# A decoder layer on one core: transfers of the attention merge issued by ScalarE, the sine product as one VectorE operation, merge work inside the waits for powers

## The chip, the cores and the metric

The kernel runs on one core of a Trainium2 chip. The metric is the device time of one execution in microseconds. Of the kernel before there are three timed runs, and one more execution that the hardware profiler recorded.

## The reference

One decoder layer over 1024 tokens of width 1024, float32. The part that matters here is mixer A, a dilated window attention with 12 query heads in three groups over 4 key/value heads:

```
qa = apply_rope(rmsnorm(qa, qn_a), cos, sin) * (HEAD_DIM_A ** -0.5)
ka = apply_rope(rmsnorm(ka, kn_a), cos, sin)
def apply_rope(t, cos, sin):
    t1, t2 = jnp.split(tf, 2, axis=-1)
    return concatenate([t1 * cos - t2 * sin, t2 * cos + t1 * sin])
for g, (window, dilation) in enumerate(((128,1), (512,4), (2048,16))):
    o, lse = dilated_group(q[:, :, g], k, v, window, dilation)
w = softmax(stack(lses), axis=0)
o = sum(w[..., None] * stack(outs), axis=0)
```

The last two lines are the merge: the three groups' outputs of a key/value head, weighted by their softmax denominators. Mixer B is a gated linear attention; both are projected, gated and added, and a SwiGLU block follows.

## The kernel before

All matrix products of float32 data are made of three products of a high and a low part (lines 2228 to 2230, helper `three`), so every weight tile is cast by ScalarE (`hi_a`, L992) and its rest taken by VectorE (`lo_a`, L1527). The program is written out for each engine, in order, with semaphores between them; a loop `Fori(1, H)` runs the attention of heads 1 to 3, and head 0 is written ahead of it.

An attention head is 16 slots, `s` = 0 to 15. In slots 0 to 7 TensorE makes a tile of q and k for four (token tile, column) pairs (`four`), in 8 to 15 it makes gate columns (`stream`). The tile of slot j goes this way:

- ScalarE squares its four parts with sums (L1077, in `act_head_a`).
- VectorE turns the sums into variances (L1679, `qk_norm`), GpSimd raises them to the power -0.5 (L730, `pool_rope`), VectorE multiplies the tile by power and gain into `qg` (L1692).
- Rotation: VectorE multiplies by the cosines (L1667) and one half by the sines (L1668), GpSimd the other half by the sines (L734); VectorE subtracts and adds (L1672, L1673).
- TensorE transposes the rotated tile behind slot j + 2 (L2367, called T(j) below), and ScalarE copies it to `qk_t` (L1095, L1098), behind its squares of slot j + 2.

From slot 6 on, the scores of a pair of blocks, their masks and negated maxima on VectorE (L1707, L1711), exponentials on ScalarE (L1119), transposes (L2328) and products with v (L2342) are put between (`UNITS_AT`).

Head h merges head h - 1 meanwhile. Its steps are: GpSimd stores the statistics to DRAM (L743) and loads them in eight small transfers in token order (`merge_stats`, L749 to L754), ahead of the power of slot 0; VectorE takes differences in slot 1 (`merge_diffs`, from L1623), ScalarE exponentials (L1065), VectorE normalises behind slot 3 (`merge_norm`); GpSimd stores the weights (L763) and, once they are stored, loads them into `wb` on all partitions (L767), between the powers of slots 3 and 4 (`merge_weights`); VectorE multiplies `wb` by the outputs (`merge_mul`, L1655) in slot 5 and twice in slot 8; GpSimd adds the three (L772, L774) and stores the sum (`merge_sum`). Head 3 is merged in the first head of mixer B, `pool_head(0, False)`.

The waits that tie the loads down are these two, and each is a wait of GpSimd's queue, with the powers behind it:

```
pool.wait_ge(stat_out, 16 * h + 16)
pool.wait_ge(wgt_out, 16 * h + 16)
```

Of the kernel before, what the change touches and what calls it, by code (L numbers as in the profile page):

```python
# [19 lines left out]
ALU = mybir.AluOpType  # L20
# [3 lines left out]
P = 128  # L24
# [10 lines left out]
def decoder_layer(nc, x_d, pos_d, norm1_d, w_in_d, qn_d, kn_d, w_up_d, b_a_d, gn_d, w_pa_d, w_pb_d,  # L35
# [256 lines left out]
    t1_gain, t1_cos, t1_sin, rot_done = sem("t1_gain"), sem("t1_cos"), sem("t1_sin"), sem("rot_done")  # L292
# [65 lines left out]

    def leave_phase(eng):
        eng.drain().then_inc(phase_end, 1)  # L360
# [11 lines left out]

    def by_tile(t, j, d=P):

        return t.rearrange("p (t m) d -> p t m d", m=2) if len(QK[j][0]) == 2 else t
# [301 lines left out]
    def _(pool):  # L677
# [60 lines left out]
        def merge_stats(h):  # L738

            sd = stat_d[bass.ds(h, 1)].rearrange("a u q -> (a u) q")  # L740
            pool.wait_ge(stat_sbd, h + 1)
            alone(pool)
            pool.dma_start(sd, stat_sb[:, :]).then_inc(stat_out, 16)  # L743
            pool.wait_ge(stat_out, 16 * h + 16)
            pool.wait_ge(c_wgt, 3 * h)
            alone(pool)
            for q in range(2):
                r0 = NU * q
                pool.dma_start(st8[:, q, 0, :], sd[r0:r0 + 8, :]).then_inc(stat_in, 16)  # L749
                for b in range(2):  # L750
                    pool.dma_start(st8[4 * b:4 * b + 4, q, 1, :].rearrange("c (r jl) -> c r jl", jl=32),
                                   sd[r0 + 8 + b:r0 + 16:2, :].rearrange("r (jh jl) -> jh r jl", jl=32)
                                   ).then_inc(stat_in, 16)
                pool.dma_start(st8[:, q, 2, :].rearrange("c (r il) -> c r il", il=16),  # L754
                               sd[r0 + 16:r0 + 24, :].rearrange("r (ih il) -> ih r il", il=16)
                               ).then_inc(stat_in, 16)

        def merge_weights(h):

            pool.wait_ge(c_wgt, 3 * h + 3)  # L760
            alone(pool)
            wd = wgt_d[bass.ds(h, 1)].rearrange("a g c t -> (a g) c t")
            pool.dma_start(wd.rearrange("g c t -> c g t"), e8[:, :, :]).then_inc(wgt_out, 16)  # L763
            pool.wait_ge(wgt_out, 16 * h + 16)
            pool.wait_ge(oa_out, 16 * h)
            alone(pool)
            pool.dma_start(wb[:, :, :], wd.rearrange("g c t -> g (c t)").partition_broadcast(P)  # L767
                           ).then_inc(wb_in, 16)
# [10 lines left out]
        for j in range(8):  # L779
            pool_rope(0, j)  # L780
# [33 lines left out]
        def pool_head(h, tail):  # L814
# [29 lines left out]
            else:  # L844
                work = ["d0", "W0", "d1", "d2", "S0", "d3"] + last
            for w in work:
# [6 lines left out]
                elif w[0] == "W":  # L853
                    merge_weights(H - 1)
# [129 lines left out]
    def _(act):  # L984
# [82 lines left out]
        def act_head_a(h, behind):  # L1067
# [4 lines left out]
            for s in range(16):  # L1072
# [26 lines left out]
                for j in UNITS_AT.get(s, []):  # L1099
# [36 lines left out]
        def act_head(h, tail):  # L1136
# [33 lines left out]
            for s in range(2 * TB):  # L1170
# [346 lines left out]
    def _(dve):  # L1517
# [139 lines left out]
        def dve_head_a(h, behind):  # L1657
            def rope(j):
# [6 lines left out]
                else:  # L1665
                    out, src = (t.rearrange("p m (a f) -> p (m a) f", a=2) for t in (r, qg[:, :, :]))
                dve.tensor_tensor(out, src, table(cos_t, j, 2), ALU.mult).then_inc(t1_cos, 1)  # L1667
                dve.tensor_tensor(by_tile(rs[:, :, 64:128], j), by_tile(qg[:, :, 0:64], j), table(sin_t, j, 1),  # L1668
                                  ALU.mult).then_inc(t1_cos, 1)
                dve.wait_ge(t1_cos, 2 * n + 2)  # L1670
                dve.wait_ge(t1_sin, n + 1)
                dve.tensor_tensor(r[:, :, 0:64], r[:, :, 0:64], rs[:, :, 0:64], ALU.subtract).then_inc(rot_done, 1)  # L1672
                dve.tensor_tensor(r[:, :, 64:128], r[:, :, 64:128], rs[:, :, 64:128], ALU.add).then_inc(rot_done, 1)  # L1673

            def qk_norm(j):
# [12 lines left out]
                dve.wait_ge(t1_sin, n)  # L1688
# [981 lines left out]
```

## Time and profile before

| | |
|---|---|
| Runs timed | 1890.19, 1892.96, 1894.15 us (median 1892.96) |
| The profiled execution | 1892.71 us |
| Its span | 1891.2 us, 27575 instructions |
| TensorE busy | 1797.0 us, 95% of the span |
| VectorE busy | 1101.1 us, 58% |
| ScalarE busy | 700.6 us, 37% |
| GpSimd busy | 551.1 us, 29% |
| Mean granted clock of TensorE | 0.99 |

The span is the time between the first and the last instruction of the profiled execution, 1.5 us less than its own time. Engines are named PE (TensorE), DVE (VectorE), ACT (ScalarE), POOL (GpSimd) and SP in the rows; L12 is a line of the kernel. A time in brackets is how long the engine stood idle before an instruction, and the arrow names what released it. Busy shares are means over stages with different limits.

### The profile page before, as it was taken

How to read it: one execution, taken by the hardware profiler on the slowest of the kernel's cores; microseconds unless marked ns; L12 is line 12 of the kernel's file. 1: busy time of each engine (PE TensorE's matmuls, PEld its weight loads, DVE VectorE, ACT ScalarE, POOL GpSimd, SP SyncE). 2: the span in 40 equal slices, each digit the busy share in tenths (PEclk: the TensorE clock that was granted, in tenths of full speed). 3: DMA queues.
4: the chain of work that ended last, by engine and by line, in shares of the span. 5: the costliest groups of instructions: out<-in, count | busy, mean ns of one | idle time of the engine just before them, and what ended most of it. 6: DMA issues, size and time to landing. Idle time of an engine off the chain costs nothing. (4 is left out here: it accounts for less than half of the span.)

```text
span 1891.2 us, 27575 instructions
## 1 busy us (share of the span) xinstructions
PE 1797.0 (95%) x9188; PEld 1521.5 (80%) x9188; DVE 1101.1 (58%) x1928; ACT 700.6 (37%) x1598; POOL 551.1 (29%) x654
## 2 busy tenths in 40 slices
PE   6999989999989899999997999999999999999999
PEld 6888877878877888888895888877888888888887
DVE  5362462562652966667576554587555555566786
ACT  5233233233243335353536222453333333334443
POOL 2020230320412705151412000006565555620120
PEclk9999999999999899999999999999999999999999
DMA  7311321421221211111015323214232323178764
GB/s 201 100 35 50 91 95 34 116 74 61 79 78 46 68 46 46 35 33 55 28 72 197 120 83 112 101 67 134 94 105 100 116 89 111 70 251 318 257 213 171
DMA packets 169173, 196.42 MB, mean 104 GB/s; under 512 B 9488, under 2 KB 119344, under 8 KB 168576
## 3 DMA queue, kind: packets, MB, share of 16 engines
q1 hardware_dynamic: 154832, 156.59, 25.9%
q0 software_dynamic: 7984, 28.29, 4.5%
q10 hardware_dynamic: 6272, 10.49, 1.5%
q8 instruction: 43, 0.70, 0.1%
q14 instruction: 42, 0.34, 0.1%
HBM read 150.88 MB, written 44.45 MB: 103 GB/s over the span
## 5 line engine op out<-in xcount | busy, mean ns | idle before, releaser
L2228 PE MATMUL bank<-act_hi,w_hi 128*128 128x512 f32 x568 | 229.1, 403 | 3.9 <-DVE act_lo L1862 3.6
L2230 PE MATMUL bank<-act_hi,w_lo 128*128 128x512 f32 x568 | 222.8, 392 | 0.0
L2229 PE MATMUL bank<-act_lo,w_hi 128*128 128x512 f32 x568 | 222.2, 391 | 0.0
L2228 PE MATMUL bank<-ca,wq 128*128 128x512 f32 x528 | 206.9, 392 | 6.7 <-DVE wq L1973 4.3
L2230 PE MATMUL bank<-ca,wq 128*128 128x512 f32 x528 | 206.0, 390 | 0.0
L2229 PE MATMUL bank<-ca,wq 128*128 128x512 f32 x528 | 205.9, 390 | 0.0
L2228 PE MATMUL bank<-w_hi,act_hi 128*128 128x256 f32 (+1 forms) x576 | 181.3, 315 | 4.0 <-DVE act_lo L1543 3.1
L2229 PE MATMUL bank<-w_lo,act_hi 128*128 128x256 f32 (+1 forms) x576 | 177.7, 308 | 0.0
L2230 PE MATMUL bank<-w_hi,act_lo 128*128 128x256 f32 (+1 forms) x576 | 177.6, 308 | 0.0
L2228 PEld LDWEIGHTS bank<-act_hi,w_hi 128*128 128x128 f32 x568 | 107.6, 189 | 27.6 <-DVE act_lo L1862 4.8
L2230 PEld LDWEIGHTS bank<-act_hi,w_lo 128*128 128x128 f32 x568 | 107.2, 189 | 23.2
L2229 PEld LDWEIGHTS bank<-act_lo,w_hi 128*128 128x128 f32 x568 | 107.5, 189 | 20.9
L2228 PEld LDWEIGHTS bank<-ca,wq 128*128 128x128 f32 x528 | 99.5, 188 | 29.8 <-issue 3.7
L1527 DVE TENSOR_TENSOR w_lo<-w_raw,w_hi 128x1024 fp32r<-128x1024 f32 x38 | 46.1, 1223 | 126.6 <-ACT w_hi L992 126.6
L2228 PEld LDWEIGHTS bank<-w_hi,act_hi 128*128 128x128 f32 x576 | 111.0, 193 | 9.4 <-issue 3.3
L2230 PEld LDWEIGHTS bank<-ca,wq 128*128 128x128 f32 x528 | 99.4, 188 | 20.7
L2229 PEld LDWEIGHTS bank<-ca,wq 128*128 128x128 f32 x528 | 99.5, 188 | 20.6
L2230 PEld LDWEIGHTS bank<-w_hi,act_lo 128*128 128x128 f32 x576 | 111.0, 193 | 5.2
L2229 PEld LDWEIGHTS bank<-w_lo,act_hi 128*128 128x128 f32 x576 | 111.1, 193 | 4.9
L1973 DVE TENSOR_TENSOR wq<-wr,wq 128x512 fp32r<-128x512 f32 x66 | 69.9, 1059 | 70.1 <-ACT wq L1361 70.1
L1361 ACT CAST wq<-tq 128x512 fp32r<-128x512 f32 x88 | 54.3, 620 | 140.2 <-PE bank L2230 118.0
L922 POOL TENSOR_TENSOR yq<-yq,sg 128x512 f32<-128x512 f32 x33 | 53.1, 1609 | 147.5 <-DVE yq L2135 59.7
(364 smaller groups left out, 4295.1 us busy)
## 6 DMA issues: line engine op xcount, KB each, us to landing
w_raw<-in_w_in SPq DMA_DIRECT2D x60, 512.0 KB, 4.0
rawd<-in_w_ffn_down SPq DMA_DIRECT2D x99, 256.0 KB, 5.0
rx<-y_scratch SPq DMA_DIRECT2D x77, 256.0 KB, 4.3
wr<-in_w_ffn_gate SPq DMA_DIRECT2D x11, 1024.0 KB, 5.5
wr<-in_w_ffn_up SPq DMA_DIRECT2D x11, 1024.0 KB, 5.4
y_scratch<-sq SPq DMA_DIRECT2D x11, 1024.0 KB, 4.3
y_scratch<-yq SPq DMA_DIRECT2D x33, 256.0 KB, 2.1
gate_scratch<-gbuf ACTq DMA_DIRECT2D x32, 256.0 KB, 2.1
```

Of the source, the lines that this page charges most:

```text
L922: pool.tensor_tensor(yq(k), yq(k), sg[:, k, :], ALU.mult).then_inc(ym_done, 1)
L1361: act.copy(wq_hi[:, w_slot(p, j), :].rearrange("p (kt n) -> p kt n", n=P), src).then_inc(whi_done, 1)
L1527: dve.tensor_tensor(w_lo[:, slot, :], w_raw[:, slot, :], w_hi[:, slot, :].bitcast(F32), ALU.subtract).then_inc(lo_done, 1)
L1973: dve.tensor_tensor(lo, src, hi.bitcast(F32), ALU.subtract).then_inc(wlo_done, 1)
L2228: pe.matmul(ps, lhs_hi, rhs_hi, start=first, stop=False, skip_group_check=onto)
L2229: pe.matmul(ps, lhs_hi, rhs_lo, start=False, stop=False, skip_group_check=onto)
L2230: return pe.matmul(ps, lhs_lo, rhs_hi, start=False, stop=last, skip_group_check=onto)
```

## The change

- The store and the eight loads of the statistics, the store of the weights and their broadcast load are issued by ScalarE: the store behind the copy that ends a head, the loads behind the squares of slot 0, the others at the end of slots 4 and 5. For head 3: in slots 0, 2 and 3 of the first head of mixer B.
- The sine product is one VectorE operation over both halves, written to `rs` in place; the subtraction and the addition read its crossed halves. GpSimd keeps the powers and the sums.
- The normalisation moves from behind the rotation of slot 3 to the wait for its power; the products from slots 5, 8, 8 to the waits in slots 6 and 7 and to slot 8.

```diff
+    def load_stats(eng, h):
+        sd = stat_d[bass.ds(h, 1)].rearrange("a u q -> (a u) q")
+        eng.wait_ge(stat_out, 16 * h + 16)
+        eng.wait_ge(c_wgt, 3 * h)
...
+    def load_weights(eng, h):
+        eng.wait_ge(wgt_out, 16 * h + 16)
+        eng.wait_ge(oa_out, 16 * h)
...
-        def pool_rope(h, j):
+        def pool_rstd(h, j):
             n = 8 * h + j
             pool.wait_ge(t1_var, n + 1)
             pool.tensor_tensor(qk_st[:, 0, j, :], qk_st[:, 1, j, :], mhalf[:, 0:4],
                                ALU.pow).then_inc(t1_rstd, 1)
-            pool.wait_ge(t1_gain, 4 * n + 4)
-            pool.wait_ge(rot_done, 2 * n)
-            pool.tensor_tensor(by_tile(rs[:, :, 0:64], j), by_tile(qg[:, :, 64:128], j), table(sin_t, j, 1),
-                               ALU.mult).then_inc(t1_sin, 1)
...
         with pool.Fori(1, H) as h:
-            merge_stats(h - 1)
-            for j in range(4):
-                pool_rope(h, j)
-            merge_weights(h - 1)
-            for j in range(4, 8):
-                pool_rope(h, j)
+            for j in range(8):
+                pool_rstd(h, j)
             merge_sum(h - 1)
         leave_phase(pool)
-        merge_stats(H - 1)
...
-                work = ["d0", "W0", "d1", "d2", "S0", "d3"] + last
+                work = ["d0", "d1", "d2", "S0", "d3"] + last
...
+                if behind and s == 0:
+                    load_stats(act, h - 1)
                 if behind and s == 1:
                     act_weights(h - 1)
+                if behind and s == 4:
+                    store_weights(act, h - 1)
+                if behind and s == 5:
+                    load_weights(act, h - 1)
...
             act.copy(stat_sb[:, :], pt_ps[0:2 * NU, 0:P]).then_inc(stat_sbd, 1)
+            store_stats(act, h)
...
+                if not tail and s == 0:
+                    load_stats(act, H - 1)
                 if not tail and s == 1:
                     act_weights(H - 1)
+                if not tail and s == 2:
+                    store_weights(act, H - 1)
+                if not tail and s == 3:
+                    load_weights(act, H - 1)
...
                 dve.tensor_tensor(out, src, table(cos_t, j, 2), ALU.mult).then_inc(t1_cos, 1)
-                dve.tensor_tensor(by_tile(rs[:, :, 64:128], j), by_tile(qg[:, :, 0:64], j), table(sin_t, j, 1),
-                                  ALU.mult).then_inc(t1_cos, 1)
+                dve.tensor_tensor(half, src, table(sin_t, j, 2), ALU.mult).then_inc(t1_cos, 1)
                 dve.wait_ge(t1_cos, 2 * n + 2)
-                dve.wait_ge(t1_sin, n + 1)
-                dve.tensor_tensor(r[:, :, 0:64], r[:, :, 0:64], rs[:, :, 0:64], ALU.subtract).then_inc(rot_done, 1)
-                dve.tensor_tensor(r[:, :, 64:128], r[:, :, 64:128], rs[:, :, 64:128], ALU.add).then_inc(rot_done, 1)
+                dve.tensor_tensor(r[:, :, 0:64], r[:, :, 0:64], rs[:, :, 64:128], ALU.subtract).then_inc(rot_done, 1)
+                dve.tensor_tensor(r[:, :, 64:128], r[:, :, 64:128], rs[:, :, 0:64], ALU.add).then_inc(rot_done, 1)
...
-                if behind and j == 5:
-                    merge_mul(h - 1, 0)
+                if behind and j == 3:
+                    merge_norm(h - 1)
+                if behind and j in (6, 7):
+                    merge_mul(h - 1, j - 6)
                 dve.wait_ge(t1_rstd, n + 1)
...
-                    if behind and s == 3:
-                        merge_norm(h - 1)
...
-                        merge_mul(h - 1, 1)
                         merge_mul(h - 1, 2)
```

What this does to the order on the engines, at three places. On ScalarE, in the loop over heads, from the squares of slot 0 to those of slot 1. Before:

```order
L1077 ACTIVATE rot,qk_st<-lvl_ps 128x128 x4
L1073 REGISTER_ALU
L1077 ACTIVATE rot,qk_st<-bank 128x128 x4
L1064 ISA
L1065 ACTIVATE e<-e 8x128
```

Now (the first half of the loads; the second half repeats it before the squares of slot 1):

```order
L1066 ACTIVATE rot,qk_st<-lvl_ps 128x128 x4
L367 ISA
L368 REGISTER_ALU
L372 ISA
L372 DMA st<-stat_scratch 8x128
L374 ISA
L374 DMA st<-stat_scratch 4x4x32
L374 ISA
L374 DMA st<-stat_scratch 4x4x32
L377 ISA
L377 DMA st<-stat_scratch 8x8x16
```

The eight loads, with the waits of L367 and L368 for the store, now stand between two squares.

On GpSimd, the top of the same loop. Before:

```order
L743 ISA
L743 DMA stat_scratch<-stat_sb 48x128
L744 ISA
L745 REGISTER_ALU
L749 DMA st<-stat_scratch 8x128
L751 ISA
L751 DMA st<-stat_scratch 4x4x32
```

Now, the end of the loop's powers and what follows them:

```order
L762 TENSOR_TENSOR qk_st<-qk_st,small 128x4
L761 REGISTER_ALU
L762 TENSOR_TENSOR qk_st<-qk_st,small 128x4
L767 ISA
L768 TENSOR_TENSOR wb<-wb 128x1024
L769 ISA
L770 TENSOR_TENSOR wb<-wb 128x1024
```

Only powers, the two sums and the store of the sum are left there.

On VectorE, slot 6 of the loop. Before:

```order
L1679 TENSOR_SCALAR qk_st<-qk_st 128x4
L1526 REGISTER_ALU
L1527 TENSOR_TENSOR w_lo<-w_raw,w_hi 128x1024
L1689 REGISTER_ALU
L1692 SCALAR_TENSOR_TENSOR qg<-lvl_ps,qk_st,k_gain 128x128
```

Now:

```order
L1681 TENSOR_SCALAR qk_st<-qk_st 128x4
L1528 REGISTER_ALU
L1529 TENSOR_TENSOR w_lo<-w_raw,w_hi 128x1024
L1646 REGISTER_ALU
L1647 ISA
L1657 TENSOR_TENSOR wb<-wb,u_t 128x1024
L1692 REGISTER_ALU
L1695 SCALAR_TENSOR_TENSOR qg<-lvl_ps,qk_st,k_gain 128x128
```

A product of the merge stands between the variances and the gains, with its wait for the broadcast (L1646, L1647); slot 7 has the same.

## Rows read from the trace of the kernel before

**Rows 1.** Waits of TensorE, whole span: waiter <- releaser: us in total, times, longest
```profile
PE lvl_ps L2367 <- DVE rot L1673: 11.6, 6, 3.1
```

**Rows 2.** Windows: length; busy us (instructions) by engine; granted clock, DMA share, GB/s
```profile
95.19:197.75 102.56, 100.33 (x542) 86.43 (x541) 42.74 (x133) 36.72 (x129) 13.48 (x12) 1.00 0.13 40
216.97:332.44 115.47, 103.98 (x541) 88.75 (x542) 57.96 (x157) 37.36 (x132) 22.72 (x19) 0.97 0.16 53
350.87:464.65 113.78, 103.86 (x541) 88.98 (x542) 57.98 (x157) 37.37 (x132) 22.73 (x19) 0.97 0.16 53
483.68:597.52 113.84, 102.39 (x541) 87.50 (x542) 57.98 (x157) 37.38 (x132) 22.72 (x19) 0.99 0.18 58
```

**Rows 3.** Timeline of GpSimd in head 1: start us, us, engine, line; idle before, releaser
```profile
207.01 0.53 POOL L749 DMA_DIRECT2D st<-stat_scratch  x1 [6.28 <-DMA stat_scratch<-stat_sb]
...
212.23 1.04 POOL L730 TENSOR_TENSOR qk_st<-qk_st,small 128x4 f32<-128x4 f32 x1
...
239.51 1.03 POOL L730 TENSOR_TENSOR qk_st<-qk_st,small 128x4 f32<-128x4 f32 x1
...
250.44 1.91 POOL L730 TENSOR_TENSOR qk_st<-qk_st,small 128x4 f32<-128x4 f32 x1 [1.24 <-DVE qk_st L1679]
...
273.70 2.39 POOL L772 TENSOR_TENSOR wb<-wb 128x1024 f32<-128x1024 f32 x1 [10.35 <-DVE wb L1655]
```

**Rows 4.** Timeline of VectorE in head 1
```profile
205.51 0.17 DVE L1679 TENSOR_SCALAR qk_st<-qk_st 128x4 f32<-128x4 f32 x1 [2.78 <-ACT rot L1077]
...
214.56 0.69 DVE L1667 TENSOR_TENSOR rot<-qg,cos_t 128x512 f32<-128x512 f32 x1
215.17 0.95 DVE L1668 TENSOR_TENSOR rs<-qg,sin_t 128x256 f32<-128x256 f32 x1
...
216.91 0.21 DVE L1623 COPY z<-st 8x128 f32<-8x128 f32 x1
...
221.92 0.41 DVE L1673 TENSOR_TENSOR rot<-rot,rs 128x256 f32<-128x256 f32 x1
...
245.62 1.23 DVE L1655 TENSOR_TENSOR wb<-wb,u_t 128x1024 f32<-128x1024 f32 x1 [1.36 <-DMA wb<-weight_scratch]
...
250.19 0.16 DVE L1679 TENSOR_SCALAR qk_st<-qk_st 128x4 f32<-128x4 f32 x1
...
269.70 3.91 DVE L1655 TENSOR_TENSOR wb<-wb,u_t 128x1024 f32<-128x1024 f32 x2
...
274.34 1.77 DVE L1711 TENSOR_SCALAR small<-stats 128x2 f32<-128x2 f32 x1
```

**Rows 5.** Timeline of TensorE: T(4) and T(7) of head 0, T(0) and T(7) of head 1
```profile
119.14 0.60 PE L2367 MATMUL lvl_ps<-ident,rot 128*128 128x128 f32 x4
...
139.89 0.38 PE L2367 MATMUL lvl_ps<-ident,rot 128*128 128x128 f32 x2
...
216.97 0.66 PE L2367 MATMUL lvl_ps<-ident,rot 128*128 128x128 f32 x4 [1.53 <-DVE rot L1673]
...
269.14 0.65 PE L2367 MATMUL lvl_ps<-ident,rot 128*128 128x128 f32 x4 [1.48 <-ACT qk_t L1095]
```

**Rows 6.** Timeline of ScalarE in head 1: squares of slots 0 and 7, one issue
```profile
204.34 0.28 ACT L1077 ACTIVATE rot<-lvl_ps 128x128 f32<-128x128 f32 x1 [3.05 <-PE lvl_ps L2230]
...
257.69 0.26 ACT L1077 ACTIVATE rot<-bank 128x128 f32<-128x128 f32 x1
...
267.08 0.36 ACTq L1084 DMA_DIRECT2D gate_scratch<-gbuf  x1
```

**Rows 7.** Windows: the normalisation of head 1; a stretch with the lower clock
```profile
231.89:235.39 3.50, 3.50 (x20) 2.94 (x19) 3.15 (x9) 0.00 (x0) 0.00 (x0) 1.00 0.00 0
306.00:312.00 6.00, 4.68 (x18) 3.90 (x17) 2.33 (x13) 2.02 (x9) 0.00 (x0) 0.72 0.00 0
```

**Rows 8.** SP's loads of weights (ns min/median/max); the statistics' loads to landing (last number, us)
```profile
L503 SPq DMA_DIRECT2D w_raw<-in_w_in x32: 367/1328/2757, 19.8 to 475.9; - x32
...
st<-stat_scratch POOLq DMA_DIRECT2D x16, 4.0 KB, 4.0
```

More of the change, by code:

```diff
@@ L291, in decoder_layer @@
     t1_sq, t1_var, t1_rstd = (sem("t1_" + n) for n in ("sq", "var", "rstd"))
-    t1_gain, t1_cos, t1_sin, rot_done = sem("t1_gain"), sem("t1_cos"), sem("t1_sin"), sem("rot_done")
+    t1_gain, t1_cos, rot_done = sem("t1_gain"), sem("t1_cos"), sem("rot_done")
     t2_ready, t2_evac = sem("t2_ready"), sem("t2_evac")
@@ L357, in alone, with store_stats, store_weights @@
         eng.sem_inc(passed, 1)
+    def store_stats(eng, h):
+        eng.wait_ge(stat_sbd, h + 1)
+        alone(eng)
+        eng.dma_start(stat_d[bass.ds(h, 1)].rearrange("a u q -> (a u) q"), stat_sb[:, :]).then_inc(stat_out, 16)
+    def load_stats(eng, h):
+        sd = stat_d[bass.ds(h, 1)].rearrange("a u q -> (a u) q")
+        eng.wait_ge(stat_out, 16 * h + 16)
+        eng.wait_ge(c_wgt, 3 * h)
+        alone(eng)
+        for q in range(2):
+            r0 = NU * q
+            eng.dma_start(st8[:, q, 0, :], sd[r0:r0 + 8, :]).then_inc(stat_in, 16)
+            for b in range(2):
+                eng.dma_start(st8[4 * b:4 * b + 4, q, 1, :].rearrange("c (r jl) -> c r jl", jl=32),
+                              sd[r0 + 8 + b:r0 + 16:2, :].rearrange("r (jh jl) -> jh r jl", jl=32)
+                              ).then_inc(stat_in, 16)
+            eng.dma_start(st8[:, q, 2, :].rearrange("c (r il) -> c r il", il=16),
+                          sd[r0 + 16:r0 + 24, :].rearrange("r (ih il) -> ih r il", il=16)
+                          ).then_inc(stat_in, 16)
+    def store_weights(eng, h):
+        eng.wait_ge(c_wgt, 3 * h + 3)
+        alone(eng)
+        eng.dma_start(wgt_d[bass.ds(h, 1)].rearrange("a g c t -> c (a g) t"), e8[:, :, :]).then_inc(wgt_out, 16)
+    def load_weights(eng, h):
+        eng.wait_ge(wgt_out, 16 * h + 16)
+        eng.wait_ge(oa_out, 16 * h)
+        alone(eng)
+        eng.dma_start(wb[:, :, :], wgt_d[bass.ds(h, 1)].rearrange("a g c t -> (a g) (c t)").partition_broadcast(P)
+                      ).then_inc(wb_in, 16)
     def leave_phase(eng):
@@ L371, in bank_a @@
         return banks[0 if s == 15 else (5, 0, 1)[s % 3]]
-    def by_tile(t, j, d=P):
-        return t.rearrange("p (t m) d -> p t m d", m=2) if len(QK[j][0]) == 2 else t
     def table(t, j, halves):
@@ L731, in pool_rope @@
                                ALU.pow).then_inc(t1_rstd, 1)
-            pool.wait_ge(t1_gain, 4 * n + 4)
-            pool.wait_ge(rot_done, 2 * n)
-            pool.tensor_tensor(by_tile(rs[:, :, 0:64], j), by_tile(qg[:, :, 64:128], j), table(sin_t, j, 1),
-                               ALU.mult).then_inc(t1_sin, 1)
[L738 to L768, printed above, removed]
         def merge_sum(h):
@@ L779, in _ @@
         for j in range(8):
-            pool_rope(0, j)
+            pool_rstd(0, j)
         with pool.Fori(1, H) as h:
-            merge_stats(h - 1)
-            for j in range(4):
-                pool_rope(h, j)
-            merge_weights(h - 1)
-            for j in range(4, 8):
-                pool_rope(h, j)
+            for j in range(8):
+                pool_rstd(h, j)
             merge_sum(h - 1)
         leave_phase(pool)
-        merge_stats(H - 1)
         enter_phase(pool, 2)
@@ L852, in pool_head @@
                     pool_o(h - 1, int(w[1]))
-                elif w[0] == "W":
-                    merge_weights(H - 1)
                 elif w[0] == "S":
@@ L1667, in rope @@
                 dve.tensor_tensor(out, src, table(cos_t, j, 2), ALU.mult).then_inc(t1_cos, 1)
-                dve.tensor_tensor(by_tile(rs[:, :, 64:128], j), by_tile(qg[:, :, 0:64], j), table(sin_t, j, 1),
-                                  ALU.mult).then_inc(t1_cos, 1)
+                half = rs[:, :, :].rearrange("p (t m) (a f) -> p t (m a) f", t=2, a=2) if len(QK[j][0]) == 2 else \
+                    rs[:, :, :].rearrange("p m (a f) -> p (m a) f", a=2)
+                dve.tensor_tensor(half, src, table(sin_t, j, 2), ALU.mult).then_inc(t1_cos, 1)
                 dve.wait_ge(t1_cos, 2 * n + 2)
-                dve.wait_ge(t1_sin, n + 1)
-                dve.tensor_tensor(r[:, :, 0:64], r[:, :, 0:64], rs[:, :, 0:64], ALU.subtract).then_inc(rot_done, 1)
-                dve.tensor_tensor(r[:, :, 64:128], r[:, :, 64:128], rs[:, :, 64:128], ALU.add).then_inc(rot_done, 1)
+                dve.tensor_tensor(r[:, :, 0:64], r[:, :, 0:64], rs[:, :, 64:128], ALU.subtract).then_inc(rot_done, 1)
+                dve.tensor_tensor(r[:, :, 64:128], r[:, :, 64:128], rs[:, :, 0:64], ALU.add).then_inc(rot_done, 1)
             def qk_norm(j):
```

1 line of the change is left out of this document (removed).

## The prediction

> **What bounds the kernel now.** I read the waits of TensorE first, then one window per attention head, then each other engine's own timeline of head 1. TensorE waits 11.6 us for the results of the rotation [rows 1], all of it in the attention stage. The windows run from the first transposes of a head, T(0), to its last product with the values. Head 0, which merges nothing, takes 102.56 us; heads 1 to 3 each merge the head before and take 115.47, 113.78 and 113.84 for the same matmuls [rows 2]. That is 12.91 + 11.22 + 11.28 = 35.4 us more. T(0) itself lies outside: the six waits for rotated tiles total 11.6, of which three, before T(4), are 3.1 each [rows 1], which leaves 2.3 for the three T(0). So at most 37.7 us hang on the merge. Part of it is clock: the granted share is 0.97, 0.97 and 0.99 in these heads against 1.00 in head 0, which is 3.5 + 3.4 + 1.1 = 8.0 us of full speed lost; a stretch with one fall to the lower level (1.2 of 2.4 GHz) shows 0.72 over 6 us, so a fall costs 1.7 [rows 2, 7].
>
> Three causes stand in GpSimd's and VectorE's rows. First, GpSimd waits 6.28 us for its store of the statistics and spends 5.2 us (207.01 to 212.23) on eight loads before it makes the powers of slot 0 [rows 3], whose input was ready at 205.51 [rows 4]. Second, in slot 4 the powers start at 239.51 [rows 3], after the normalisation of 3.50 us [rows 7], a store of the weights, its landing and the issue of the broadcast; T(4) waits 3.1. Third, the sum on GpSimd (273.70, 2.39 us) holds a VectorE operation on two numbers for 1.77 us, until GpSimd ends [rows 3, 4]; ScalarE's exponentials and the transposes behind them wait.
>
> **The change part by part.** *Transfers.* Eleven issues per head leave GpSimd: one store goes behind the last copy of ScalarE's head, eight loads behind its squares of slot 0, the weights' store behind slot 4 and the broadcast behind slot 5. ScalarE's own issues take 0.36 [rows 6]; there is no row of it issuing several in sequence, so I bound one from below by 0.36 and from above by the slowest of SP's, 2.757 (median 1.328) [rows 8], and take 0.4, nearest to its own queue. The loads then occupy ScalarE for 3.2 us from 205.5. The next squares come a slot later: T(0) unhindered is 216.97 - 1.53 = 215.44 and slot 0's squares start at 204.34, so a slot is (215.44 - 204.34) / 2 = 5.5, and squares(1) are due at 209.9 [rows 5, 6]. 205.5 + 3.2 = 208.7: hidden, with 1.2 to spare. The statistics land 4.0 later [rows 8]. From the first merge operation to the end of rope(1) is 222.3 - 216.9 = 5.4 [rows 4], less 0.35 for the sine (below) 5.05. So rope(1) ends at 205.5 + 3.2 + 4.0 + 5.05 = 217.8, and T(1) is due at 221.0 at the earliest. With a cost c per issue this is 214.55 + 8c: free up to c = 0.8. The T(0) wait goes; the powers of slots 0 and 4 no longer stand behind transfers. The broadcast took 6.7 us from its issue (about 238.9) to the merge product that waited for it (245.62) [rows 3, 4]; the product, now in slot 6, comes a slot (5.5) and the cast and split of a weight tile (some 2, an estimate) after the issue, so the broadcast just lands in time.
>
> The Trainium skill, DMA: Bandwidth & Descriptors, Issuing engines are not separate DMA queues, says that transfers run on the same 16 DMA engines whoever issues them, and that only the sequencer's time is saved, usually small beside the transfer. By it the landings above stay, as I left them; what is not small here is that the sequencer also holds the powers.
>
> *Sine.* VectorE's second half product (256 elements) takes 0.95 behind a cosine product of 512 that is passed in 0.61 (214.56 to 215.17) [rows 4]. One product of 512 should take as long as the cosine: 0.99 becomes 0.61 to 0.65, so 0.35 less in each of 32 steps, and a GpSimd operation less. In head 0 it is worth nothing: no wait there is for a rotated tile. In heads 1 to 3 it shortens the chain that follows.
>
> *Products and normalisation in the waits for the powers.* Slot 3 gets the 3.50 before its gains instead of behind its rotation. Slots 0 to 5 have more than 3 us between the end of a rotation and its transposes (217.8 against 221.0 above), so I cost it at nothing; without that cover it is 3.5 minus one power of 1.04. Slots 6 and 7 are another matter: there VectorE, ScalarE and the scores form one loop. From T(4): the transposes 0.66 and the squares 1.17 (204.34 to 205.51), 1.83 [rows 4 to 6]. From there, 250.19, to the squares of slot 7, 257.69, now 7.50; less 0.35, plus the first product 1.23, 8.4 [rows 4, 6] (the power of 1.91, held up by the split of a weight tile, becomes one of 1.04, but the split now waits for its cast; I set one against the other). From 257.69 to T(7), 269.14, 11.45; less 0.35, plus the second product 3.91 / 2 = 1.95, 13.05 [rows 4 to 6]. Sum 23.3. Head 0 has T(4) to T(7) in 139.89 - 119.14 = 20.75 [rows 5]. T(7) will wait 2.5 us. The sums on GpSimd start earlier, but again meet the small operations of slots 8 and 9: 0 to 1.6 (1.77 less 0.17), I take 0.9. So 3.4 per head stay, 10.2 in all. Of the clock I keep a fall in every second head, 1.5 x 1.7 = 2.5, for a wait of 2.5 us is still there.
>
> *Last merge,* at the start of the second mixer: GpSimd gets its stream 4.1 earlier (normalisation to power, 235.4 to 239.5, in head 1 [rows 3, 7]); against this, the statistics arrive later, behind ScalarE's first activations: 8 x 0.36 = 2.9 of issue. I take 0, and keep -4 to +4.
>
> **Sum:** 37.7 - 10.2 - 2.5 = 25.0 less. The profiled execution took 1892.71 (median of the runs 1892.96, the same within 0.02%): 1892.7 - 25.0 = 1867.7, I say 1868.
>
> **The rivals.** *The chain does not bind* (0.07): the loop of slots 6 and 7 has hidden slack, the clock stays up; all 37.7 go: 1855.
> *VectorE's merge work shuts out the powers* (0.12): the power next to a split took 1.91 instead of 1.04 [rows 3]. If the products of slots 6 and 7 hold up the power as the split did, 0.87 in each, 3 x 2 x 0.87 = 5.2 come back: 1873. For it is that row; against it, the split now waits for a cast that gives the power its time. The Trainium skill, SBUF — State Buffer, Who interferes with whom, says that a VectorE operation with two SBUF inputs and a GpSimd one that reads SBUF exclude each other for the whole instruction. By that rule alone work put into a wait for a power hides nothing, which speaks against this part of the change.
> *ScalarE issues at SP's median* (0.10): 1.33 each is 0.53 over the free 0.8; 8 x 3 x 0.53 = 12.7: 1880.
> *ScalarE issues slower still* (0.06), slower than before: from c = 0.8 + 25.0 / 24 = 1.84 the loads of slot 0 delay squares(1), the statistics and T(1) by more than all the rest wins. At 2.757 it is 24 x 1.96 = 47 back: 1915. For it: SP's rows reach it while it loads values and weights, in the same microseconds. Against it: ScalarE's stores hold at 0.36 in that traffic.
> *The wait only moves* (0.03): T(7) or the scores behind it take up what T(0) and T(4) lose, 1893. It would need 11 us at one point in each head; the chain above gives 2.5.
>
> **How the numbers follow.** The forecast has 0.62, within 1861 to 1875 (residue 1 to 5.5 per head, clock 0 to 5 in all, last merge 4 either way). A measurement here tells 0.2% (3.8 us) from no change. Faster: 0.62 + 0.07 + 0.12 + 0.10 = 0.91; within 0.2%: 0.03; slower: 0.06. From 1856 to 1881 lie nearly all of the forecast, the powers' rival and most of the 1880 case, 0.8 together.
>
> **What would show it.** Right: no TensorE wait before T(0) and T(4) in heads 1 to 3; heads of about 106 us; the power 0.1 us behind its input in every slot; a sine product like the cosine's 0.69; ScalarE's eight loads done before its squares of slot 1; a wait of 2 to 3 us before T(7). Wrong: issues on ScalarE over 0.8; a power of 2 us in slot 6 or 7; a product of slot 6 that waits for the broadcast; a larger wait before the first level products of the second mixer.

## The result and the profile after

The changed kernel takes 1881.55 us (median of 4 runs, 1880.51 to 1882.80) against 1893.36 for the kernel before: ratio 0.994, 95% interval 0.9924 to 0.9956. It is 11.8 us faster where 25 were forecast. The time lies 6.55 us above the forecast's range of 1861 to 1875, and 0.55 us above the 1881 up to which the prediction had put 0.8 of its chances. (In what follows, two numbers in brackets behind a time are the 95% interval of its ratio to the kernel before, which was timed again beside each group of runs.) Its profiled execution took 1880.51 us. The head of its page (span; busy us, share of the span and instructions of each engine):

```profile
span 1878.8 us, 27431 instructions
PE 1793.7 (95%) x9188; PEld 1521.5 (81%) x9188; DVE 1090.1 (58%) x1928; ACT 701.5 (37%) x1598; POOL 485.3 (26%) x578
```

GpSimd lost 66 us of busy time: the half products 37.7, its 44 DMA issues 25.7, and 2.7 by shorter powers. VectorE is busy 11 us less; TensorE and ScalarE changed by 3.3 us at most.

Waits of TensorE in the changed kernel (engine, line, what it waited for: us in total, times, longest), against [rows 1]:

```profile
PE bank L2228 <- DVE w_lo L1529: 11.9, 2, 6.1
PE lvl_ps L2423 <- DVE lvm L1789: 8.3, 5, 4.9
PE lvl_ps L2367 <- ACT qk_t L1084: 6.5, 3, 2.2
...
PE bank L2341 <- DVE u_t L1720: 2.0, 3, 0.9
```

The six waits for rotated tiles (11.6 us) are gone. The wait before T(7) stands where it was forecast, 2.2 us a head. The first row is new: twice TensorE waits some 6 us for a split weight tile.

Windows of the changed kernel: first the heads 0 to 3, from T(0) to the last product with the values, as in [rows 2], then the three stretches between them (us, then busy time and count of PE, PEld, DVE, ACT, POOL, granted clock, DMA share, GB/s):

```profile
96.52:199.04 102.52, 100.30 (x542) 86.44 (x541) 40.82 (x133) 36.77 (x129) 6.05 (x6) 1.00 0.13 40
216.58:323.90 107.32, 102.25 (x542) 87.74 (x541) 55.32 (x154) 37.53 (x132) 11.44 (x9) 0.98 0.17 57
348.97:455.64 106.67, 100.86 (x543) 86.33 (x542) 52.53 (x145) 36.67 (x129) 11.48 (x9) 1.00 0.17 57
481.48:588.20 106.72, 100.91 (x542) 86.32 (x541) 52.52 (x145) 36.66 (x129) 11.46 (x9) 1.00 0.19 62
199.04:216.58 17.54, 17.54 (x127) 16.52 (x125) 6.91 (x15) 5.13 (x20) 2.02 (x2) 1.00 0.83 229
323.90:348.97 25.07, 19.29 (x127) 18.07 (x125) 9.91 (x25) 5.92 (x23) 2.05 (x2) 0.86 0.58 160
455.64:481.48 25.84, 19.75 (x126) 18.53 (x125) 9.91 (x25) 5.92 (x23) 2.04 (x2) 0.87 0.58 155
```

Heads 1 to 3 fell from 343.09 us to 320.71, 22.4 less. The stretches between heads, by the bounds of [rows 2], were 19.22, 18.43 and 19.03; they are now 17.54, 25.07 and 25.84. The first shows what they should be, for the wait before T(0) is gone; the other two are 7.5 and 8.3 longer than it, 15.8 in all. That is the missing gain: 11.8 measured plus 15.8 is 27.6, against 25.0 forecast.

What happens there, on ScalarE (timeline; in brackets the idle time before an instruction and its releaser; ACTq rows are its DMA issues). First the passage from head 0 to head 1, then from head 1 to head 2:

```profile
200.31 0.26 ACT L1120 COPY stat_sb<-bank 48x128 f32<-48x128 f32 x1 [0.49 <-ACT gbuf L1071]
200.68 0.35 ACTq L362 DMA_DIRECT2D stat_scratch<-stat_sb  x1
201.32 2.00 ACT L981 CAST w_hi<-w_raw 128x1024 fp32r<-128x1024 f32 x2 [0.75 <-ACT stat_sb L1120]
...
325.35 0.26 ACT L1120 COPY stat_sb<-bank 48x128 f32<-48x128 f32 x1 [0.66 <-ACT gbuf L1071]
326.12 0.38 ACTq L362 DMA_DIRECT2D stat_scratch<-stat_sb  x1
332.65 1.04 ACT L981 CAST w_hi<-w_raw 128x1024 fp32r<-128x1024 f32 x1 [7.05 <-issue]
```

Both passages do the same work, but in the second ScalarE's jump lies between the store and the cast, the jump from the end of its loop over heads to its start (head 0 is written out in front of the loop). The idle 7.05 us has no releaser, only "issue". The split of that tile and the TensorE group that waits for it follow, and the granted clock over the stretch is 0.86:

```profile
336.14 0.58 PE L2228 MATMUL bank<-w_hi,act_hi 128*128 128x256 f32 x1 [5.78 <-DVE w_lo L1529]
```

The DMA view of the changed kernel, from the copy's end to the restart (325.61 to 332.65), shows two packets of a queue that carries instructions (queue, kind: packets, MB, share of 16 engines):

```profile
q1 hardware_dynamic: 3327, 1.68, 83.0%
q10 hardware_dynamic: 208, 0.29, 11.0%
q14 instruction: 2, 0.02, 0.6%
```

The trace's packet records put them at 329.7 and 330.7, of 8192 bytes each, in the middle of the traffic of the V loads (the loads of the values `vt`), which SyncE issued from 324.67 on. The 16 DMA engines are 95% busy in this window.

### The profile page after: what moved, and what is told of

It reads as the page before. It is cut to its first block and busy times, and to the rows that moved or that the text cites. A ratio compares the mean times of both kernels' runs of the same rounds, so it can differ in the third digit from the quotient of the medians.

```text
span 1878.8 us, 27431 instructions
## 1 busy us (share of the span) xinstructions
PE 1793.7 (95%) x9188; PEld 1521.5 (81%) x9188; DVE 1090.1 (58%) x1928; ACT 701.5 (37%) x1598; POOL 485.3 (26%) x578
## 5 line engine op out<-in xcount | busy, mean ns | idle before, releaser
L762 POOL TENSOR_TENSOR qk_st<-qk_st,small 128x4 f32<-128x4 f32 x32 | 32.4, 1011 | 389.3 <-DVE qk_st L1681 389.3
L2230 PEld LDWEIGHTS bank<-act_hi,w_lo 128*128 128x128 f32 x568 | 107.3, 189 | 23.2
```

Of the source, the lines that this page charges most:

```text
L2230: return pe.matmul(ps, lhs_lo, rhs_hi, start=False, stop=last, skip_group_check=onto)
```

## Experiments

Three theories stood at the start. A: ScalarE must fetch code after the jump, and the fetch stands behind the V and weight loads. B: the loop body has grown so that a fetch is needed at all (the instructions that the compiler makes for ScalarE, counted from its first one, have the loop at 294 to 555 before the change and at 298 to 597 after it; in the traces, from one jump to the next, ScalarE executes 261 and 299). C: the store at the loop's end, by its wait or its queue, holds ScalarE.

**Who issues the store, and where.** First the store went back to GpSimd alone:

```diff
-            store_stats(act, h)
         with pool.Fori(1, H) as h:
+            store_stats(pool, h - 1)
             for j in range(8):
...
+        store_stats(pool, H - 1)
```

> The changed kernel with one thing undone: the store of the statistics goes back from ScalarE to GpSimd (ahead of its powers of the next head; one more behind its last head). The changed kernel stands at 1881.6. Theory C (the store itself, its wait or its queue, holds ScalarE 7 us at the end of its loop body): the idle of 7.05 and 7.36 us before the first cast of heads 2 and 3 goes, TensorE's 5.8 and 6.1 us before the first weights of slot 1 go, and with their restart about 15 us: 1866 to 1869. Theory A (ScalarE must fetch the code at its loop's start, and the fetch stands behind the V and weight loads, which SyncE issued 1.8 us earlier): the jump comes only 0.4 us earlier, so most of the idle stays, 4 to 7 us a head: 1876 to 1882. Theory B (the longer loop body no longer lies in the engine's instruction memory, so that a fetch is needed at all): the body is three instructions shorter, the idle stays: 1880 to 1882.

Measured 1868.71 us (0.9858 to 0.9893). ScalarE in that kernel:

```profile
326.27 0.26 ACT L1122 COPY stat_sb<-bank 48x128 f32<-48x128 f32 x1 [0.66 <-ACT gbuf L1073]
326.80 2.00 ACT L983 CAST w_hi<-w_raw 128x1024 fp32r<-128x1024 f32 x2 [0.28 <-issue]
```

The stall is gone. Taken alone this run says C. The next keeps the store on ScalarE, but away from the jump:

```diff
             hi_a(3, 2 * h + 2)
+            if behind:
+                store_stats(act, h - 1)
...
-            store_stats(act, h)
```

(and one store for the last head behind the loop).

> The changed kernel, its store of the statistics still on ScalarE but behind the two casts at the start of the next head, so that the copy of the statistics ends the loop body as in the kernel before. Theory C: idle gone, 1866 to 1869 (the store comes 2.5 us later, the statistics still land before the squares of slot 1 are over). Theories A and B: the jump comes 0.4 us earlier and the body has the same length: the idle of 4 to 7 us before the first cast stays, 1876 to 1882. If the idle stays here and in the run with GpSimd's store, the store is innocent.

Measured 1881.24 (0.9922 to 0.9958): 6.77 and 6.82 us idle between the copy and the cast, with no store between them. C falls. What is left between the two kernels is small: both bodies begin at compiled instruction 296, and the jump is instruction 591 in the first and 594 in the second. So either three more instructions of length count, which is B as it was put, or the place where the jump lies, which no theory had in it.

**The traffic.** On SyncE the V loads were held back until ScalarE's two casts were done:

```diff
             sp.wait_ge(pv_ready, NB * h)
+            alone(sp)
+            sp.wait_ge(hi_done, A0 + TA * h + 4)
             load_vt(h)
```

> The changed kernel with one wait more on SyncE: the three V loads of a head start behind ScalarE's two casts at the start of the head, so that nothing that SyncE issues stands in the way of ScalarE at its jump; ScalarE's code is that of the changed kernel. Theory A: the fetch lands at once, the idle shrinks to 1 to 2 us: 1868 to 1872. Theory B: a fetch is still needed, but whether it costs 7 us or 1 depends on what it shares the queues with; with A it gives 1868 to 1872, alone 1880. Theory C (the store's issue or wait): the idle of 7 stays, 1880 to 1882.

Measured 1873.78 (0.9883 to 0.9919), between what A and what C had given. The restart:

```profile
328.97 1.99 ACT L983 CAST w_hi<-w_raw 128x1024 fp32r<-128x1024 f32 x2 [3.79 <-issue]
```

The first packet of the instruction queue now comes 1.0 us behind the copy's end instead of 4.1, and the idle shrinks from 7.05 to 3.79. Without the V loads (the DMA engines are 23% busy in this window) the fetch still costs 3.5 us more than the 0.3 of a jump that does not stall, and the V loads ahead of it double that: A holds for half of the stall. The other half is there with little traffic, so the question of B is the one that decides.

**No jump.** ScalarE's heads 1 to 3 written out:

```diff
-        with act.Fori(1, H) as h:
+        for h in range(1, H):
             act_head_a(h, True)
```

> The changed kernel with ScalarE's loop over heads 1 to 3 written out, so that its code runs on without a jump; everything else, the store's place too, is kept. Theories A and B: no jump, the code is fetched ahead, the idle before the first casts of heads 2 and 3 goes and with it about 15 us: 1866 to 1869. Theory C: the store still ends each head, the idle of 7 us stays: 1880 to 1882.

Measured 1863.41 (0.9827 to 0.9862), 2.6 us under what was expected without a stall, with the store at each head's end and the V loads at their place; the cast follows the copy by 0.55 and 0.83 us.

**Position or length.** ScalarE got increments of a semaphore that nobody reads, ahead of its loop, where it waits anyway. They move the loop in the instruction stream and change nothing in it (24 at each of two places in the run moved by 48, shown here, fewer in the other three):

```diff
         hi_a(1, 2)
+        for _ in range(24):
+            alone(act)
         v_out(7)
...
             hi_a(3, 2 * h + 2)
+            if not behind:
+                for _ in range(24):
+                    alone(act)
             for s in range(16):
```

> The changed kernel with 48 increments of a semaphore that nobody reads, on ScalarE where it waits ahead of its loop (24 ahead of its last V tile, 24 ahead of the squares of head 0). Nothing else changes; the loop body, with the store at its end, is the same 302 instructions of the compiled stream, at 346 to 645 in place of 298 to 597. Theory B in the form that the first four runs leave (what counts is where the body's ends lie against a boundary of the instruction memory that falls between 591 and 594, and a multiple of 128 or 256 instructions from it): the body now lies like that of the kernel with GpSimd's store, no idle at the jump, 1864 to 1869. If the body's length alone counts (295 is short enough, 298 is not), the idle of 7 us in heads 2 and 3 stays: 1880 to 1883.

> The kernel whose store of the statistics is on GpSimd (1868.7), with ten such increments on ScalarE ahead of its loop, which then jumps at instruction 601 in place of 591. Position decides: the idle of 4 to 7 us before the first casts of heads 2 and 3 appears although ScalarE issues no store there: 1878 to 1884. Length decides, or the store: 1867 to 1870.

> The kernel before with 39 such increments ahead of ScalarE's loop: body at 333 to 594 in place of 294 to 555, otherwise untouched. Position decides: idle before the first casts of heads 2 and 3, some 12 to 16 us slower than the kernel before: 1905 to 1909. Length decides (262 instructions are few), or only the store: 1893.

> The changed kernel with 20 such increments ahead of ScalarE's loop (body at 318 to 617, still on both sides of the boundary and reaching back beyond the next one): a control, for the increments themselves. Position decides: idle as in the changed kernel, 1880 to 1883. If any shift cured it: 1864 to 1869.

(298 to 597 is 300 instructions, not the 302 of the first expectation.) Measured: 1865.79 (0.9840 to 0.9873), 1876.00 (0.9886 to 0.9919), 1907.79 (1.0058 to 1.0092) and, from two runs, 1883.63 (0.9926 to 0.9965). Two of the times miss what was expected for position by about 2 us (1876.00 against 1878 to 1884) and 0.6 us (1883.63 against 1880 to 1883), but the idle time that tells the theories apart is there in both. The same change is worth 12 us or 28 according to 48 instructions that do nothing, and 39 of them cost the kernel before 14 us. ScalarE in the three that decide, the changed kernel moved by 48:

```profile
325.30 0.35 ACTq L362 DMA_DIRECT2D stat_scratch<-stat_sb  x1
326.21 2.00 ACT L981 CAST w_hi<-w_raw 128x1024 fp32r<-128x1024 f32 x2 [1.14 <-issue]
```

GpSimd's store, moved by 10 (no store of ScalarE's here, yet the stall):

```profile
324.89 0.26 ACT L1127 COPY stat_sb<-bank 48x128 f32<-48x128 f32 x1 [0.66 <-ACT gbuf L1078]
329.76 1.99 ACT L983 CAST w_hi<-w_raw 128x1024 fp32r<-128x1024 f32 x2 [4.61 <-issue]
```

and the kernel before, moved by 39 (a second idle of 3.65 us follows within its loop):

```profile
333.61 0.26 ACT L1130 COPY stat_sb<-bank 48x128 f32<-48x128 f32 x1 [0.67 <-ACT gbuf L1087]
340.09 1.04 ACT L992 CAST w_hi<-w_raw 128x1024 fp32r<-128x1024 f32 x1 [6.22 <-issue]
344.79 1.04 ACT L992 CAST w_hi<-w_raw 128x1024 fp32r<-128x1024 f32 x1 [3.65 <-issue]
```

Length alone falls, for 300 instructions stall or not by their place, and 262 can be made to. One run more asked which places are bad. The changed kernel was moved by 140 (24 at each of five V tiles, 20 ahead of head 0's squares):

> The changed kernel with 140 increments of the unused semaphore on ScalarE ahead of its loop (24 ahead of each of its last five V tiles, 20 ahead of the squares of head 0): body at 438 to 737. Counted from the boundary found between 591 and 594, blocks of 128 instructions begin at about 336, 464, 592 and 720, and the body touches four of them, as in every run with a stall; blocks of 256 begin at about 336, 592 and 848, and it lies in two of them, as in every run without. If the engine keeps whole blocks of 256, no idle at the jump in heads 2 and 3: 1864 to 1869 (up to 3 more if the increments delay the V tiles). If it keeps blocks of 128 (the fetches seen are of 8192 bytes, 128 instructions), the idle of about 7 us is back: 1879 to 1884.

Measured 1881.51 (0.9921 to 0.9955); ScalarE:

```profile
325.99 0.35 ACTq L362 DMA_DIRECT2D stat_scratch<-stat_sb  x1
332.05 1.04 ACT L981 CAST w_hi<-w_raw 128x1024 fp32r<-128x1024 f32 x1 [6.28 <-issue]
```

The stall is back. That excludes blocks of 256, and blocks of 128 fit, with starts at 336, 464, 592 and 720 (each could be up to 2 later). Every run falls into line:

| kernel | loop in ScalarE's stream | blocks touched | idle, heads 2 and 3 | us |
|---|---|---|---|---|
| before | 294 to 555 | 3 | 0.29, 0.27 | 1893.4 |
| GpSimd's store | 296 to 591 | 3 | 0.27, 0.25 | 1868.7 |
| changed, moved by 48 | 346 to 645 | 3 | 1.14, 1.10 | 1865.8 |
| changed | 298 to 597 | 4 | 7.05, 7.36 | 1881.6 |
| store in the next head | 296 to 594 | 4 | 6.77, 6.82 | 1881.2 |
| V loads late | 298 to 597 | 4 | 3.80, 3.73 | 1873.8 |
| GpSimd's store, moved by 10 | 306 to 601 | 4 | 4.61, 4.82 | 1876.0 |
| before, moved by 39 | 333 to 594 | 4 | 6.22, 6.67 | 1907.8 |
| changed, moved by 20 | 318 to 617 | 4 | 7.28, 6.75 | 1883.6 |
| changed, moved by 140 | 438 to 737 | 4 | 6.28, 6.65 | 1881.5 |

The idle time is from the end of the copy of the statistics to the next cast. Counting alone does not fix the size: blocks of 64, of which a loop may touch five, give the same split of the ten rows. The size of the packets speaks for 128 (that 8192 bytes are 128 instructions rests on the page of the Trainium skill cited in the last section). The packet records tie the stall to the fetch. In each of the 14 stalled passages of the table a packet of 8192 bytes on the instruction queue q14 began 1.76 to 2.05 us before the cast that ended the idle time. In the passages without a stall there was none, or it was one for which ScalarE did not wait (in the kernel before, one at 334.19 us was still under way when the cast began at 334.45). The queue is not ScalarE's alone: it has packets where ScalarE makes no jump, so a packet by itself does not say whose code it brings. Why the stall is 4.6 in one run and 7 in others was not followed up.

**The terms of the prediction, one at a time.** The first two of these runs have the loop where the kernel moved by 48 has it, and no stall at the jump (1.1 us idle in both). The first undoes the sine part (a half product back on GpSimd) in the kernel moved by 48:

```diff
+            pool.wait_ge(t1_gain, 4 * n + 4)
+            pool.wait_ge(rot_done, 2 * n)
+            pool.tensor_tensor(by_tile(rs[:, :, 0:64], j), by_tile(qg[:, :, 64:128], j), table(sin_t, j, 1),
+                               ALU.mult).then_inc(t1_sin, 1)
...
-                dve.tensor_tensor(half, src, table(sin_t, j, 2), ALU.mult).then_inc(t1_cos, 1)
+                dve.tensor_tensor(by_tile(rs[:, :, 64:128], j), by_tile(qg[:, :, 0:64], j), table(sin_t, j, 1),
+                                  ALU.mult).then_inc(t1_cos, 1)
```

> The changed kernel with the 48 increments ahead of ScalarE's loop (1865.8, no stall at the jump), and the sine product split again: one half on GpSimd behind the power, one on VectorE, as before. By the prediction's 0.35 per slot in the loop of slots 6 and 7, 0.7 a head come back, 2.1, and up to 0.9 more in a slot where GpSimd's half stands before a power: 1867 to 1871. If the sine matters in every slot of the merging heads (0.35 x 8 x 3 = 8.4): 1874. If it is hidden: 1866.

Measured 1869.29 (0.9859 to 0.9889), 3.5 slower than 1865.79. The two were timed at different times and their intervals overlap, so the 3.5 is rough, and the rows say more. VectorE in slot 6 and TensorE's wait before T(7):

```profile
247.20 0.96 DVE L1683 TENSOR_TENSOR rs<-qg,sin_t 128x256 f32<-128x256 f32 x1
248.19 0.42 DVE L1687 TENSOR_TENSOR rot<-rot,rs 128x256 f32<-128x256 f32 x1
```

```profile
PE lvl_ps L2381 <- ACT qk_t L1097: 8.1, 3, 2.7
```

0.99 us from one start to the next, against 0.72 with the full product (209.97 to 210.69, below): 0.27 a slot. T(7) waits 8.1 us in all instead of 6.5, 0.53 a head, which is twice 0.27: only slots 6 and 7 count, as the loop of the prediction has it. That gives 1.6 of the 3.5. The rest is not explained. Most of it stands in the second merging head (109.1 us against 107.4 in the kernel moved by 48), but that head is as long (108.9) in the profiled execution of the next run, whose median is no higher, and both show a clock of 0.97 there against 0.98. So it may be no effect of the sine.

The second puts the normalisation back behind the rotation of slot 3:

```diff
-                if behind and j == 3:
-                    merge_norm(h - 1)
...
                     rope(s)
+                    if behind and s == 3:
+                        merge_norm(h - 1)
```

> The changed kernel with the 48 increments ahead of ScalarE's loop (1865.8), and the normalisation back behind the rotation of slot 3. The prediction costed this move at nothing: VectorE then starts slot 4 up to 1.9 us late (231.5 + 3.5 against an input at about 233.1 for its first small operation when slot 4's squares of 229.1 are done at 230.3), ends its rotation by 238.5, and T(4) is due after 240: 1865 to 1867. If the three slots behind have less room than that, up to 3.5 a head come back: up to 1876.

Measured 1865.51 (0.9834 to 0.9867): no difference that shows, as costed.

The last two test the residue before T(7) and are meant to beat both kernels: ScalarE's loop written out, and the merge moved so that its products leave the loop of slots 6 and 7.

```diff
-                if behind and j == 3:
+                if behind and j == 2:
                     merge_norm(h - 1)
-                if behind and j in (6, 7):
-                    merge_mul(h - 1, j - 6)
+                if behind and j == 5:
+                    merge_mul(h - 1, 0)
+                    merge_mul(h - 1, 1)
...
-                if behind and s == 4:
+                if behind and s == 3:
                     store_weights(act, h - 1)
-                if behind and s == 5:
+                if behind and s == 4:
                     load_weights(act, h - 1)
```

> ScalarE's loop written out (1863.4, no jump), and the merge moved earlier: the normalisation into the wait for the powers of slot 2, the weights' store behind slot 3 and the broadcast behind slot 4, and both products of slots 6 and 7 into the wait of slot 5. Theory: the 2.0 to 2.2 us that TensorE still waits before T(7) in heads 1 to 3 (6.1 in all) are the two products in the loop of slots 6 and 7, as the prediction worked out; slot 5 has room for them, since its tile is due two slots later. T(7) waits go: 1856 to 1859. If another step sets T(7) (power, exponentials), they stay, 1863. If the broadcast lands after slot 5's powers are ready (store at about 224.5, landing 2 to 6, issue at the earliest 230, landing 6.3: 236.5 against the input of slot 5 at 236.2), VectorE waits up to 1 us there, which the slot hides.

The other differs in `if behind and j in (5, 6): merge_mul(h - 1, j - 5)`.

> As the run with both products in slot 5, but the second in slot 6 (where the first one was): one product of 1.99 us left in the loop of slots 6 and 7 in place of 1.22 + 1.99. By the products' theory T(7) waits 0.7 to 1.0 a head: 1859 to 1861. If the wait for T(7) is not made by the products it stays at 2.0 in this run and in the other, 1863.

Measured: 1852.89 (0.9774 to 0.9801) with both products in slot 5, 1859.19 (0.9804 to 0.9831) with one in slot 6. TensorE's wait before T(7) goes from 6.1 us (both in the loop) over 3.0 (one) to none. The heads of the first, windows as above:

```profile
96.63:199.13 102.50, 100.31 (x543) 86.44 (x541) 40.87 (x133) 36.72 (x129) 6.04 (x6) 1.00 0.12 39
216.66:319.54 102.88, 100.51 (x543) 86.41 (x542) 52.80 (x146) 36.62 (x129) 12.49 (x9) 1.00 0.18 60
337.07:439.64 102.57, 100.41 (x543) 86.43 (x542) 53.98 (x149) 36.71 (x130) 12.48 (x9) 1.00 0.18 59
457.17:560.02 102.85, 100.41 (x543) 86.43 (x542) 54.40 (x151) 37.11 (x131) 12.48 (x9) 1.00 0.19 64
```

A head that merges now takes 0.1 to 0.4 us longer than head 0, which does not merge. The run beats its expectation (1856 to 1859). Against the written-out kernel (1863.41) it is 10.5 us faster: the waits for T(7) are 6.1 of that and those for the values' results 2.0 (2.3 to 0.3), and the rest was not followed.

This run also tests a rival of the prediction, that a product in the wait for a power shuts the power out. VectorE and GpSimd in slot 5:

```profile
236.50 3.17 DVE L1657 TENSOR_TENSOR wb<-wb,u_t 128x1024 f32<-128x1024 f32 x2
236.56 2.04 POOL L762 TENSOR_TENSOR qk_st<-qk_st,small 128x4 f32<-128x4 f32 x1 [4.91 <-DVE qk_st L1681]
```

The power takes 2.04 us instead of 1.01 beside the first product, in each of the three heads, and again in the run with one product in slot 5. It costs nothing here, because the power still ends (238.60) before the second product does (239.67).

## Why the prediction was wrong

**The step that failed** is the first term of "The change part by part", the transfers. Moving eleven issues a head to ScalarE was priced by the time that they hold its queue (0.4 us each, hidden), and everything else that they bring was put at nothing without a reason. What was not counted is code. The store, eight loads, the weights' store and the broadcast add 38 compiled instructions to ScalarE's loop body, which then touches four blocks of 128 instead of three. The jump back to its start waits for a fetch, 7.05 and 7.36 us in place of 0.3. With the same body moved by 48 instructions the stall is gone, and the kernel is 15.8 us faster (1881.55 less 1865.79). The prediction asked of each issue what it delays on its queue, but not what it does to the code around it. None of the rivals had this: the one at 1880 (ScalarE issues at SyncE's median) comes near the time by luck, and its mechanism is refuted below. "The wait only moves" is right in kind, for a new wait did appear at one point of a head, but it had T(7) or the scores in mind and not the head's start.

**What was right,** by the kernel moved by 48, in which that step costs nothing: 1865.8 against a forecast of 1867.7. Its three merging heads:

```profile
216.61:323.36 106.75, 100.93 (x542) 86.32 (x541) 54.81 (x152) 37.34 (x132) 11.47 (x9) 1.00 0.18 58
341.03:448.42 107.39, 102.30 (x542) 87.66 (x541) 54.38 (x151) 37.17 (x131) 11.44 (x9) 0.98 0.17 56
466.05:572.78 106.73, 100.91 (x542) 86.33 (x541) 54.73 (x152) 37.27 (x132) 11.46 (x9) 1.00 0.19 62
```

They take 22.2 us less than the 343.09 of the kernel before, and the three stretches ahead of them (17.54, 17.67, 17.63) take 3.8 less: 26.1, against the 25.0 of the sum. One head still shows a clock under 1.00, 0.98 or some 2 us of full speed, against 2.5 kept.

*Transfers.* No wait before T(0) or T(4) is left. GpSimd in head 1 of the changed kernel (against [rows 3]) no longer has issues in its stream:

```profile
207.06 1.01 POOL L762 TENSOR_TENSOR qk_st<-qk_st,small 128x4 f32<-128x4 f32 x1 [75.31 <-DVE qk_st L1681]
...
232.53 1.01 POOL L762 TENSOR_TENSOR qk_st<-qk_st,small 128x4 f32<-128x4 f32 x1 [5.71 <-DVE qk_st L1681]
...
268.60 2.40 POOL L770 TENSOR_TENSOR wb<-wb 128x1024 f32<-128x1024 f32 x1
```

Each power takes 1.01 us and the one of slot 0 starts 0.08 behind its input (206.81 + 0.17), as VectorE's rows say (against [rows 4]):

```profile
206.81 0.17 DVE L1681 TENSOR_SCALAR qk_st<-qk_st 128x4 f32<-128x4 f32 x1 [2.05 <-ACT rot L1066]
...
209.36 0.69 DVE L1669 TENSOR_TENSOR rot<-qg,cos_t 128x512 f32<-128x512 f32 x1
209.97 0.69 DVE L1672 TENSOR_TENSOR rs<-qg,sin_t 128x512 f32<-128x512 f32 x1
210.69 0.42 DVE L1674 TENSOR_TENSOR rot<-rot,rs 128x256 f32<-128x256 f32 x1
...
215.93 0.21 DVE L1625 COPY z<-st 8x128 f32<-8x128 f32 x1 [2.37 <-DMA st<-stat_scratch]
```

The eight loads on ScalarE (against [rows 6]; the first and the last of them, and the squares of slot 1):

```profile
208.10 0.56 ACTq L372 DMA_DIRECT2D st<-stat_scratch  x1
...
211.76 0.28 ACTq L377 DMA_DIRECT2D st<-stat_scratch  x1
212.21 0.28 ACT L1066 ACTIVATE rot<-bank 128x128 f32<-128x128 f32 x1 [5.44 <-PE bank L2230]
```

They take 3.9 us, 0.49 each, against 0.4 taken and 0.8 allowed; VectorE takes the statistics up 4.2 behind the start of the last issue, against 4.0. So ScalarE issues neither at SyncE's median nor slower, and both rivals on it fall. But the loads are not hidden "with 1.2 to spare". They begin 1.3 us behind the end of the squares, and squares(1), 0.17 behind the last of them, start at 212.21. In the written-out kernel with both products in slot 5, whose squares of slot 0 start at the same 205.63, the eight take 2.9 us (from 206.54 to 209.47) and squares(1) start at 211.39. The loop form thus holds squares(1) 0.8 us, with two register instructions of ScalarE's ahead of each load. T(1) had room for it and did not wait.

*Sine.* 0.27 us a slot, against 0.35; its product now equals the cosine's 0.69.

*Residue.* T(7) waits 2.2, against 2.5, and the products are its cause. Heads of 106.7 to 107.3 in the changed kernel, against "about 106". The rival by which VectorE's products shut out the powers did not come into play: the powers of slots 6 and 7 too took 1.01, since VectorE reaches its product at 244.43, behind the split, when the power that began at 242.60 is over. Its mechanism is real, though, as the 2.04 us of the power beside a product in slot 5 show. The Trainium skill's rule of exclusion (SBUF — State Buffer, Who interferes with whom) was thus not tested by the changed kernel itself, and that power agrees with it. The prediction's reading that by this rule work in a wait for a power hides nothing goes too far: with both products in slot 5 the second one hides what the first held up. GpSimd's sums still hold VectorE's two-number operation for 1.75 us, twice a head, as before the change.

*Normalisation* at nothing and the broadcast landing in time for slot 6: both held.

*Last merge.* Taken as 0; the longest wait before the mixer's level products fell from 7.3 to 4.9, and all of them together from 10.5 to 8.3 (8.6 in the kernel moved by 48), so it gave about 2. Its broadcast did not land in time: VectorE's first product there waited 3.95 us for it.

## What to carry to other kernels

When a change puts instructions into an engine's loop, or ahead of it, count the compiled loop body and ask which blocks of its stream it touches; here, on ScalarE, three blocks of 128 ran through and a fourth cost 4 to 7 us at every jump. The mark in a trace is an idle time with no releaser ("issue") at the first instruction of a loop body, with packets of an instruction queue inside it. If it stands on the critical path, write the loop out (1863.41 us here) or move it with idle instructions ahead of it (1865.79), and test any change beside a copy whose loop lies elsewhere before judging what the change itself is worth.

## What the hardware showed that was not expected

- The jump's fetch comes as packets of 8192 bytes (128 instructions), and the data traffic holds them up: the first came 4.1 us behind the copy's end with the V loads ahead, 1.0 without them. Idle times at the same jump were 0.3 us where ScalarE waited for no fetch (1.1 with a DMA issue ahead of the jump), 3.8 with a fetch and no V load, 4.6 to 7.4 with both.
- The Trainium skill, Runtime: NRT & Kernel Launch, Instruction fetch mechanics, says that the instruction memory has two lines of 16 KiB (256 instructions each), filled in sequence, and that a taken branch whose target lies outside them must wait for a fetch. The traces agree that it waits, and for a fetch. They do not agree on the lines: the body moved by 140 lies in two blocks of 256, by the boundary that the other nine kernels give, and waited 6.28 us; blocks of 128, of which a loop may touch three, fit all ten kernels of the table.
- Issues on ScalarE's queue, eight in sequence between 208.10 and 212.04, follow each other by 0.49 us. In the same microseconds SyncE issued four weight tiles (from 202.44 to 211.13), which took it 8.7 us, and single ones took up to 2.757 in the kernel before [rows 8].
- A GpSimd power of 128x4 took 2.04 us instead of 1.01 where it began 0.06 us behind a VectorE product of 128x1024 with two inputs in SBUF, and 1.01 beside merge operations on 8 partitions, which also took no longer than alone.
